# Most halves of the down projection as seven products of quarter sums, summed in HBM

## What is computed

```
up = causal_depthwise_conv(h @ w_up[l], conv_w[l], conv_b[l])
gate, val = jnp.split(up, 2, axis=-1)
y = (jax.nn.gelu(gate, approximate=True) * val) @ w_down[l]
x = x + rmsnorm(y, post_ffn_g[l])
```

## Time and profile before

| | us |
|---|---|
| median of 3 runs | 2617.95 (2617.83 to 2619.63) |
| the profiled execution: its own time | 2616.87 |
| its span, first to last instruction | 2615.1 |
| PE busy | 2598.0 (99%) |
| DVE busy | 1890.7 (72%) |
| ACT busy | 1145.9 (44%) |
| POOL busy | 197.1 (8%) |

### The profile page before, as it was taken

How to read it: one execution, slowest core, us unless ns; L and a number is a source line. 1 busy time by engine, 2 the same in 40 slices (tenths; PEclk the granted TensorE clock), 3 DMA queues, 4 the chain that set the end, 5 groups by cost and what they waited for, 6 DMA issues and landing times.

```text
span 2615.1 us, 44288 instructions
## 1 busy us (share of the span) xinstructions
PE 2598.0 (99%) x18036; PEld 2433.3 (93%) x18036; DVE 1890.7 (72%) x2673; ACT 1145.9 (44%) x1540; POOL 197.1 (8%) x273
## 2 busy tenths in 40 slices
PE   9999999999999999999999999999999999999998
PEld 8999999999999888888999999999999999999997
DVE  7897888788878545336787667677676767677777
ACT  8543434443444322234454444444444444444443
POOL 0100000000000100000001111111111111111111
PEclk9999999999999999999999999999999999999999
DMA  6434343343343833434236555555555555555567
GB/s 243 142 120 138 114 141 112 115 126 118 105 153 119 327 130 129 152 129 153 81 112 143 138 140 134 134 138 137 137 130 138 135 132 137 135 132 144 130 147 271
DMA packets 107659, 372.03 MB, mean 142 GB/s; under 512 B 12448, under 2 KB 12448, under 8 KB 101584
## 3 DMA queue, kind: packets, MB, share of 16 engines
q1 hardware_dynamic: 72864, 264.28, 31.6%
q0 software_dynamic: 34608, 105.06, 18.2%
HBM read 297.98 MB, written 67.11 MB: 140 GB/s over the span
## 4 chain that ended last, share of the span: by engine, by line
PE 95%; DVE 3%; issue 1%; DMA 0%; ACT 0%; DVEq 0%; SPq 0%; ACTq 0%
PE ps L643 31%; PE ps L645 31%; PE ps L644 31%; PE ps L735 1%; PE ps L682 1%; PE ps L725 1%; DMA w_raw<-in_w 0%; PE ps L709 0%; DVE w_hl L1643 0%; DVE big L2101 0%; DVE w_hl L1636 0%; DVE w_hl L2042 0%; DVE h_lo L2206 0%; DVE mixing L1697 0%; DVE w_hl L2036 0%
## 5 line engine op out<-in xcount | busy, mean ns | idle before, releaser
L643 PE MATMUL ps<-h_hi,w_hl 128*128 128x256 f32 (+1 forms) x2032 | 611.8, 301 | 4.1 <-DVE w_hl L2042 2.2
L645 PE MATMUL ps<-h_hi,w_hl 128*128 128x256 f32 (+1 forms) x2032 | 605.5, 298 | 0.0
L644 PE MATMUL ps<-h_lo,w_hl 128*128 128x256 f32 (+1 forms) x2032 | 605.4, 298 | 0.0
L643 PE MATMUL ps<-w_hl,h_hi 128*128 128x512 f32 (+1 forms) x1168 | 433.6, 371 | 2.8 <-DVE w_hl L1643 2.2
L644 PE MATMUL ps<-w_hl,h_hi 128*128 128x512 f32 (+1 forms) x1168 | 429.4, 368 | 0.0
L645 PE MATMUL ps<-w_hl,h_lo 128*128 128x512 f32 (+1 forms) x1168 | 429.1, 367 | 0.0
L643 PEld LDWEIGHTS ps<-h_hi,w_hl 128*128 128x128 f32 x2032 | 388.6, 191 | 19.9 <-DVE w_hl L1643 3.3
L644 PEld LDWEIGHTS ps<-h_lo,w_hl 128*128 128x128 f32 x2032 | 388.6, 191 | 13.3 <-issue 1.0
L645 PEld LDWEIGHTS ps<-h_hi,w_hl 128*128 128x128 f32 x2032 | 388.5, 191 | 11.4
L1093 ACT ACTIVATE w_hl<-w_raw 128x768 fp32r<-128x768 f32 x152 | 128.6, 846 | 446.8 <-PE ps L645 446.7
L1349 ACT ACTIVATE w_hl<-w_raw 128x768 fp32r<-128x768 f32 x168 | 142.1, 846 | 405.1 <-PE ps L645 405.1
(11 more groups left out here) (272 smaller groups left out, 5636.0 us busy)
## 6 DMA issues: line engine op xcount, KB each, us to landing
w_raw<-in_w SPq DMA_DIRECT2D x487, 512.0 KB, 3.5
y_scratch<-work POOLq DMA_DIRECT2D x160, 256.0 KB, 6.0
gate_scratch<-mixing POOLq DMA_DIRECT2D x8, 1024.0 KB, 6.8
mixing<-in_x POOLq DMA_DIRECT2D x4, 1024.0 KB, 6.9
mixing<-mixing POOLq DMA_DIRECT2D x16, 256.0 KB, 3.5
merged<-gate_scratch POOLq DMA_DIRECT2D x4, 1024.0 KB, 14.9
g_ret<-gate_scratch POOLq DMA_DIRECT2D x4, 1024.0 KB, 13.9
y_scratch<-work POOLq DMA_DIRECT2D x8, 512.0 KB, 20.9
```

What stands on the lines that cost most here:

```text
L643: pe.matmul(bank, s_hi, m_hi_, start=first, stop=False, skip_group_check=skip)
L644: pe.matmul(bank, s_hi, m_lo_, start=False, stop=False, skip_group_check=skip)
L645: return pe.matmul(bank, s_lo, m_hi_, start=False, stop=last, skip_group_check=skip)
```

## The change

18 of the 20 loop halves (groups 1 to 9) do their part of `w_down` as quads too. A half's four down chunks become two subs of two quads (`down_quads`); each sub gives seven products of 256 by 512 outputs, held in seven PSUM banks, in 84 matmuls of 256 columns. The last two loop halves and the group after the loop stay plain.

- ACT copies seven banks a sub, 14 a half instead of 8, to five staging tiles (`leave_product`), and POOL adds each to its own 256 KB place in `y7_scratch`, which holds seven products for each of four column blocks. In group 1 the DMA writes instead of adding, and the zeroing is gone.
- After the 17th and 18th half, 14 DMAs from HBM to HBM, 512 KB each, add the products up to the four quarters of the output (`sum_products`, in levels that wait for one another); the plain halves after that and the final loads work on those.
- DVE makes quad sums and splits for four more chunks a half, and once a group four sums of activation quarters (`make_forms`) and their splits. `quad_round` now runs through all twelve chunks of a half, with the other work hung between rounds. The first five adds of `recombine` (`u_early`) come ahead of round 9 of a half (rounds are counted from 0, round 8 being the first of the down part) and the last two (`u_last`) inside it.
- POOL's area for its DMAs' descriptors shrinks to 2048 bytes a partition, which frees SBUF for the fifth staging tile and the new operands.

```diff
+QUAD_HALVES = HALVES - 2
+QUAD_GROUPS = QUAD_HALVES // 2
+SUB = 2
+STAGES = 5
...
+SUB_BANKS = ((7, P1, Q6, P2, Q7, Q4, Q3), (Q5, 7, P1, Q6, P2, Q7, Q4))
+LEAVE = ((0, 1, 2, 3, 4, 5, 6), (0, 2, 3, 4, 5, 6, 1))
+AFTER_SUBS = (Q3, Q5, P1, Q6, P2, Q7, Q4)
+C11, C12, C21, C22 = P2, Q3, Q4, Q7
...
-            pool.memset(zeros, 0.0).then_inc(zeros_set, 1)
-            pool.wait_ge(zeros_set, 1)
-            for t in range(TT):
-                for c in range(2):
-                    pool.dma_start(y_dram[t, :, c * 1024:c * 1024 + 1024], zeros).then_inc(y_cleared, 16)
-            pool.wait_ge(y_cleared, 16 * 2 * TT)
...
+            def accumulate_products(g, e):
+                for sub in range(SUB):
+                    for j, k in enumerate(LEAVE[sub]):
+                        n = left_before(half_index(g, e)) + 7 * sub + j
+                        pool.wait_ge(y_left, n + 1)
+                        target = y7_dram[SUB * e + sub, ORDER[k]]
+                        if g == 1:
+                            pool.dma_start(target, staged[n % STAGES]).then_inc(y_added[n % STAGES], 16)
+                        else:
+                            pool.dma_start(target, staged[n % STAGES], accum_op=ALU.add)\
+                                .then_inc(y_added[n % STAGES], 16)
...
+            def accumulate_plain(e, dd):
                 for t in range(TT):
-                    pool.wait_ge(y_left, 8 * h + 4 * dd + t + 1)
-                    pool.dma_start(y_dram[t, :, d * NB:d * NB + NB], staged[t], accum_op=ALU.add)\
-                        .then_inc(y_added[t], 16)
-            for h in range(HALVES - 1):
-                for dd in range(2):
-                    accumulate(h, dd)
+                    n = left_before(QUAD_HALVES + e) + 4 * dd + t
+                    pool.wait_ge(y_left, n + 1)
+                    rows = slice(t % 2 * HB, t % 2 * HB + HB)
+                    left, right = ((C11, C12), (C21, C22))[t // 2]
+                    target = y7_dram[SUB * e + dd, left:right + 1:right - left, :, rows].rearrange("a p s -> p a s")
+                    pool.dma_start(target, staged[n % STAGES].rearrange("p (a s) -> p a s", a=2), accum_op=ALU.add)\
+                        .then_inc(y_added[n % STAGES], 16)
+            sum_levels = (((C11, P1), (Q6, P1)), ((C22, Q6), (C12, Q6)), ((C21, C22), (C12, Q5)), ((C22, Q5),))
...
+            def sum_products(e, level):
+                for to, other in sum_levels[level]:
+                    pool.dma_start(y7_dram[SUB * e:SUB * e + SUB, to], y7_dram[SUB * e:SUB * e + SUB, other],
+                                   accum_op=ALU.add, max_dma_last_dim=8192).then_inc(products_summed, 16)
...
+            for g in range(1, QUAD_GROUPS + 1):
+                for e in range(2):
+                    accumulate_products(g, e)
+                    if (g, e) == (QUAD_GROUPS, 0):
+                        added(left_before(QUAD_HALVES - 1))
+                        sum_products(0, 0)
+                        pool.wait_ge(products_summed, 16 * 2)
+                        sum_products(0, 1)
+            added(left_before(QUAD_HALVES))
+            pool.wait_ge(products_summed, 16 * 4)
+            sum_products(0, 2)
+            sum_products(1, 0)
+            pool.wait_ge(products_summed, 16 * 8)
+            sum_products(0, 3)
+            sum_products(1, 1)
+            pool.wait_ge(products_summed, 16 * 11)
+            for dd in range(2):
+                accumulate_plain(0, dd)
+            sum_products(1, 2)
+            pool.wait_ge(products_summed, 16 * 13)
+            sum_products(1, 3)
+            pool.wait_ge(products_summed, 16 * 14)
...
+            def down_quads(c, s, w, act_count):
+                pe.wait_ge(act_lo, act_count)
+                e, left = s * 7 - 7, left_before(w)
+                waits = (((y_left, left), (p1_left, s), (u_step, e + 1), (u_step, e + 2), (u_step, e + 3),
+                          (u_step, e + 4), (u_step, e + 5)),
+                         ((u_step, e + 7),) + tuple((y_left, left + k) for k in range(1, 7)))
+                for sub in range(SUB):
+                    for i in range(SUB):
+                        pe.wait_ge(lo_ready, c + SUB * sub + i + 1)
+                        w_h, w_l = quad_split(i)
+                        for k, p in enumerate(ORDER):
+                            if i == 0 and (waits[sub][k][0] is not y_left or waits[sub][k][1]):
+                                pe.wait_ge(*waits[sub][k])
+                            bank, col = ps[SUB_BANKS[sub][k]], slice(COLUMN[p] * HB, COLUMN[p] * HB + HB)
+                            o_h, o_l = down_operand(p, i)
+                            for m in range(2):
+                                tok = slice(m * P, m * P + P)
+                                mm = passes(bank[:, m * HB:m * HB + HB], (o_h[:, tok], o_l[:, tok]),
+                                            (w_h[:, col], w_l[:, col]), i == 0 and m == 0, i == SUB - 1, True)
+                            if i == SUB - 1 and k < 6:
+                                mm.then_inc(y_done, 1)
+                        mm.then_inc(chunk_used, 1)
...
+            def leave(n, bank, scale=1.0):
+                if n >= STAGES:
+                    act.wait_ge(y_added[n % STAGES], 16 * (n // STAGES))
+                act.activation(staged[n % STAGES], bank, ACT.Copy, scale=scale).then_inc(y_left, 1)
...
+            def leave_product(g, e, sub, j):
+                w, k = half_index(g, e), LEAVE[sub][j]
+                if k < 6:
+                    act.wait_ge(y_done, done_before(w) + 6 * sub + k + 1)
+                else:
+                    act.wait_ge(chunk_used, half_chunk_0(g, e) + KH + SUB * sub + SUB)
+                leave(left_before(w) + 7 * sub + j, ps[SUB_BANKS[sub][k]][:, :], -1.0 if ORDER[k] in (Q4, Q5) else 1.0)
...
+                tasks = {**tasks, KH: lambda: leave_p1(s), KH + 1: lambda: gate_linear(g, e),
+                         KH + 2: lambda: [leave_product(g, e, 0, j) for j in range(5)],
+                         KH + 3: lambda: (val_linear(g, e), leave_product(g, e, 0, 5), leave_product(g, e, 0, 6)),
+                         KH + 4: lambda: ([leave_product(g, e, 1, j) for j in range(3)], gelus(s)),
+                         KH + 5: lambda: [leave_product(g, e, 1, j) for j in range(3, 7)]}
+                for i in range(2, PER_HALF + 2):
+                    quad_hi(c, i, c + (i - 1))
+                    quad_sum_hi(n + i, i)
+                    if i in tasks:
+                        tasks[i]()
...
+            def quad_round(c, n, i, ahead=None, between=(None, None)):
+                ahead = i + 1 < KH if ahead is None else ahead
+                if between[0]:
+                    between[0]()
                 if ahead:
                     quad_sum_one(c, n + 1, i + 1)
                 raw_lo_of(c, i)
+                if between[1]:
+                    between[1]()
                 if ahead:
                     quad_sum_two(n + 1, i + 1)
                 sums_lo_of(n, i)
...
+            def u_early(s, c):
+                dve.wait_ge(p1_left, s)
+                TTm(c12, u_bank(s, c, Q6), c11, ALU.subtract).then_inc(u_step, 1)
+                TTm(c11, u_bank(s, c, P2), c11, ALU.add).then_inc(u_step, 1)
+                dve.wait_ge(u_step, s * 7 - 6)
+                TTm(c22, u_bank(s, c, Q7), c12, ALU.add).then_inc(u_step, 1)
+                dve.wait_ge(u_step, s * 7 - 4)
+                TTm(c21, u_bank(s, c, Q4), c22, ALU.subtract).then_inc(u_step, 1)
+                TTm(c12, u_bank(s, c, Q3), c12, ALU.add).then_inc(u_step, 1)
+            def u_last(s, c):
+                dve.wait_ge(u_step, s * 7 - 2)
+                TTm(c12, u_bank(s, c, Q5), c12, ALU.add).then_inc(u_step, 1)
+                TTm(c22, u_bank(s, c, Q5), c22, ALU.add).then_inc(u_step, 1)
...
+                between = {KH + 1: (lambda: u_early(s, c), lambda: u_last(s, c))}
+                tasks = {**tasks, KH + 2: lambda: gate_taps(g, e), KH + 4: lambda: val_taps(g, e),
+                         KH + 5: lambda: products(s, e)}
+                for i in range(2, PER_HALF + 2):
+                    quad_round(c, n + i, i, True, between.get(i, (None, None)))
+                    if i in tasks:
+                        tasks[i]()
...
+            def form_tasks(g, e):
+                if e:
+                    return {}
+                return {2: lambda: first_forms_lo(g - 1), 3: lambda: make_forms(g - 1),
+                        5: lambda: second_forms_lo(g - 1)}
...
-    nc = bacc.Bacc("TRN2", target_bir_lowering=False, num_devices=1)
+    nc = bacc.Bacc("TRN2", target_bir_lowering=False, num_devices=1, dynamic_dma_scratch_size=2048)
```

(37 more changed lines are left out.)

229 lines of the change are left out of this document (149 added, 80 removed).

## The result

The changed kernel takes 2886.86 us (median of 4 runs, 2882.37 to 2892.96), the kernel before 2618.3 in the same runs. The ratio is 1.1026, 95% interval 1.1000 to 1.1052. The direction was forecast, the size was not: 241 us beyond the forecast of 2646, 197 beyond the end of the range.

What follows compares the result with a forecast made beforehand. PE, busy 99% of the span, was taken as the bound. 2616.9 - 29.4 (PE's saving) + 21 (recombination) + 1 (activation pieces) + 29 (staging) + 6 (HBM sums) + 1 (ends) = 2645, or 2646 us on the median; 80% range 2606 to 2690.

Steps and rivals of the forecast that it cites:

- Six levels at that price: HBM sums after the 17th and 18th halves: levels priced at 21 us each, waits around the 18th half, +6 us.
- the zeroing's 20.9 us: Landing time of the old kernel's queued 512 KB zeroing DMA, taken as the price of the HBM sums.
- 40 us of up projection hide a level: HBM sums, lower bound: at 2.6 us of transfer plus 5 of latency nothing, hidden behind the up projection.
- Rival (d): HBM sums run on few DMA engines, levels of 25 us, 2664 us in all; chance 0.21.
- The rule of the Trainium skill that stood behind it: HBM sums: engine count is the largest up to 16 dividing both sides' slowest dimension, here 2.
- What PE saves: Down part of 18 halves: 168 short matmuls take 20.16 us in place of 21.79, -29.4 us.
- rival (b): Whole kernel: nothing waits at all, DVE included, 2589 us; chance 0.07.
- The recombination: PE waits 1.1 to 1.2 us for DVE's low part at chunk 9 of each of 18 halves, +21 us.
- Staging: First up chunk of the next half: PE waits for copies held by DMA landings, 1.8 us in 16 halves, +29.
- Rival (a): Loop staging: landings hold, copies never wait, only the recombination costs, 2611 us; chance 0.20.
- Rival (c): Loop: the DMA queue is the bound, 4 to 7 us of waiting a half, 2680 to 2730 us; chance 0.12.
- Anatomy of one DMA: Staging DMAs: skill rule of about 2.0 us plus bytes at 436 GB/s, 2.6 us for 256 KB; no copy would wait.

Runs made afterwards that it cites:

- e_area: Changed kernel with four staging tiles instead of five and POOL's descriptor area at 4096 bytes a partition instead of 2048: 2823.5 us, one run.
- e_nosum: Changed kernel without the 14 sums in HBM and the waits on them (output lacks those additions): 2651.1 us, ratio 1.0127.
- e_spread: Changed kernel with each of the 14 sums in HBM cut in 32 outermost pieces instead of 2: 2654.4 us, ratio 1.0144.
- e_write_between: `e_write` with `u_last` back inside round 9, as in the changed kernel: 2614.9 us, ratio 0.9990.
- e_write: `e_both` with every group writing its products to HBM instead of adding (output lacks the sums over groups): 2598.2 us, ratio 0.9924.
- e_ulast: `e_spread` with `u_last` moved behind the third sum of round 9 instead of ahead of its second: 2659.7 us, ratio 1.0169.
- e_both: `e_spread` with `u_last` moved as in `e_ulast` and seven staging tiles as in `e_seven`: 2654.4 us, ratio 1.0129.
- e_seven: `e_spread` with copies 12 and 13 of each half in two more staging tiles, in unused `u_val`: 2637.1 us, ratio 1.0077.
- e_four: `e_spread` with four staging tiles instead of five: 2703.9 us, ratio 1.0327.

## Why the prediction was wrong

The step that failed is "Six levels at that price". It took 21 us for a level; a level of two sums took 54, that of four 100. Four assumptions in it were wrong.
- That the DMAs of a level run together. POOL is held for 22 to 26 us in the issue of a further sum, 9 times; with twice the area, 3 times (`e_area`).
- That the smaller area for descriptors costs nothing. The sum has no term for it.
- That the zeroing's 20.9 us was a fair price. It was near for one sum (23.7) by accident: the zeroing was queued, this is a transfer on two engines. In 32 pieces it is 8.7.
- That 40 us of up projection hide a level. The copies of the next half stand in the same queue behind the levels, so a late level stops PE within that half. The term measured 236 us (the changed kernel less `e_nosum`) where it had +6, and 232 of them go with the shape (less `e_spread`).

Rival (d) named the right mechanism at 0.21, but priced it at 25 us a level and +24 us in all. Even where a part of the sums overlap, it is +120 (`e_area`). The rule of the Trainium skill that stood behind it was the only thing that spoke of this shape. The row of the zeroing did not, and the sum should not have gone by its time as if a level were one transfer.

The loop's terms were right in kind. By `e_write_between` and `e_write`, less the kernel before:
- What PE saves: forecast -1.63 a half, -29.4. A half in `e_write` takes 60.8 us, so -1.3 and -23. Its down part takes 20.50 us, not 20.16, most of the rest in the first steps of the second sub (0.33 and 0.22 us). With no waits at all (rival (b)) the kernel takes 2598, not 2589.
- The recombination: PE's step is as counted, 1.13 us over the usual 0.12 in 16 of 18 halves and more in the first and the last. Its worth is 16.6 us where nothing else binds (forecast 21), and nothing beside the additions, where the wait behind the copies takes its place (`e_ulast`).
- Staging: forecast 1.8 us in 16 halves, +29. Measured 64.08 - 61.74 (the half of `e_write_between`) = 2.3, +37. The place was right, the first chunk of the next half, and so was the releaser. The median landing of 7.3 us lies in the forecast's "over 6.5". Rival (a) falls: landings do not hold. Rival (c), the queue as bound, has the better picture of why: its price, 4 to 7 us a half, was 1.7 to 3 times too high.
- The estimate by Anatomy of one DMA in the Trainium skill's "DMA: Bandwidth & Descriptors", 2.6 us for 256 KB, does not hold here, beside the weight loads and one another: additions landed after 7.3 us in the median, the DMAs of `e_write`, nearly all plain writes, after 4.7 to 6.3 by tile.

Together the loop lost 33 us net (`e_nosum`) where the prediction had +22. With the sums as cheap as it took them, 2646 would have stood against 2654, in part because the errors of the loop's terms (+6, -4 and +8) have different signs. The direction, slower, would have come true by the loop alone.

Still open: which two engines carry a sum of two pieces, since the rows don't name engines; why the doubled area let one pair out together and held the next; and how the 232 us divide between few engines and held issues, of which `e_area` shows only that both count. That DMA engines are the limit in the 20 us rests on the share of 1.04 and on `e_write`, in which the issues on POOL got shorter too, so what of the gain is theirs stays open; that lowering the traffic by degrees gives the time back by degrees was not tried.

## To carry to other kernels

Before a DMA from HBM to HBM is costed, look at the outermost dimension of its access: the same 512 KB landed in 23.7 us in 2 pieces and in 8.7 in 32, a change of a few words of code and of 232 us. Ask of every DMA what is queued behind it on its issuing engine, and whether two of them fit its descriptor area. An addition in HBM is paid in DMA packet time, here 0.86 us of all 16 engines more than a write of 256 KB. Where such DMAs come in bunches, seven staging tiles for five gave back 17 us of 37, and 1.13 us a half saved ahead of the bunch was worth nothing. Before a saved wait is counted as a gain, see whether it makes another one longer, and whether the granted clock falls in it.

## What the hardware showed

- An issue on POOL can block without a semaphore: 22 to 26 us until the DMA before had gone, with 2048 bytes a partition for descriptors.
- A DMA of 512 KB from HBM to HBM in 2 pieces moved 64 packets of 8192 bytes, two at a time, and 448 packets of 8 bytes; in 32 pieces the 448 were gone and up to 16 and a few more of the 64 ran at a time.
- Around steps of 2.3 us and more PE's granted clock was at 0.50 for 3 to 7 us in nine of 12 halves (`e_both`); in `e_seven`, with steps of 2.1 us at the most, never; in `e_four` eight times, six of them after steps of 1.7 to 2.2 us.
- An addition of 256 KB from SBUF moved in packets of 2048 bytes and a write in packets of 4096, 64 packets fewer; POOL's issue took 0.85 us and 0.54.
